# Wide column blocks in the query and gate rounds of an input projection, and one silu step for the gates

## The reference

```
h = rmsnorm(x, g_mix_pre)                       # (256, 2048)
proj = h @ w_in                                 # (2048, 8208)
mq, mk, mv, mo, mi, mf, rq, rk, rv, rg = split(proj)
mq, mk = silu(causal_dwconv(mq, mk))            # 8 mLSTM heads: convolution, silu
hm = mlstm(mq, mk, mv, mi, mf)                  # gate rows mi, mf: 8 columns each
hm = head_rmsnorm(hm, g_mlstm_head) * sigmoid(mo)
rq, rk = rotary(rq), rotary(rk)                 # 8 retention heads: rotated
hr = head_rmsnorm(retention(rq, rk, rv), g_ret_head) * silu(rg)
x = x + rmsnorm(concat(hm, hr) @ w_out, g_mix_post)
x = x + rmsnorm(swiglu_ffn(rmsnorm(x)), g_ffn_post)
```

## Time and profile before

| | |
|---|---|
| Median of 3 runs | 1235.89 us (1235.27 to 1236.32) |
| The profiled execution | 1238.89 us, of which the span of its instructions is 1237.2 us |
| PE busy | 1222.7 us, 99% of the span |
| DVE busy | 717.1 us, 58% |
| ACT busy | 599.3 us, 48% |
| DMA | 229.49 MB, mean 185 GB/s over the span |
| Mean granted clock of PE | 0.996 of full |

### The profile page before, as it was taken

One profiled execution on the slowest core, in us unless ns is written; L12 is line 12 of the kernel. 1 busy time (PEld: TensorE's weight loads), 2 busy tenths in 40 slices (PEclk: granted clock), 3 DMA queues, 4 the chain that ended last, 5 costly groups with the idle time before them and its releaser, 6 DMA issues.

```text
span 1237.2 us, 15798 instructions
## 1 busy us (share of the span) xinstructions
PE 1222.7 (99%) x5899; PEld 1026.1 (83%) x5899; DVE 717.1 (58%) x923; ACT 599.3 (48%) x789; POOL 14.2 (1%) x35
## 2 busy tenths in 40 slices
PE   8999999999999999999999999999999999999997
PEld 7888888888888888888888888888888888888886
DVE  6656778776777656744554554454455454544544
ACT  5654666574554645644444444444444444443442
POOL 2000100000000000000000000000000000000000
PEclk9999899999999999999999999999999999999999
DMA  8666798867887556465656565555656565556551
GB/s 313 208 145 165 132 213 171 146 166 163 204 179 187 200 178 214 157 193 181 194 180 203 175 198 190 183 192 184 200 173 200 188 220 203 182 192 204 186 188 69
DMA packets 136937, 229.49 MB, mean 185 GB/s; under 512 B 6080, under 2 KB 55488, under 8 KB 136384
## 3 DMA queue, kind: packets, MB, share of 16 engines
q1 hardware_dynamic: 136608, 226.84, 62.8%
q0 software_dynamic: 288, 2.10, 0.4%
HBM read 226.83 MB, written 2.10 MB: 185 GB/s over the span
## 4 chain that ended last, share of the span: by engine, by line
PE 90%; DMA 4%; DVE 3%; ACT 1%; issue 0%; SPq 0%; DVEq 0%; ACTq 0%
PE bank L1252 89%; DMA raw<-in_w_in 4%; DVE w_lo L779 1%; PE bank L1536 1%; DMA resid<-in_x 1%; ACT w_hi L441 1%; PE bank L1257 0%; PE bank L1454 0%; DVE gT L993 0%; ACT L604 0%; DVE h L806 0%; DVE resid L1124 0%; PE bank L1509 0%; DVE pre L966 0%; DVE hT L792 0%
## 5 line engine op out<-in xcount | busy, mean ns | idle before, releaser
L779 DVE TENSOR_TENSOR w_lo<-raw,w_hi 128x1024 fp32r<-128x1024 f32 x420 | 512.9, 1224 | 481.8 <-ACT w_hi L441 481.3
L441 ACT ACTIVATE w_hi<-raw 128x1024 fp32r<-128x1024 f32 x420 | 443.5, 1060 | 569.4 <-PE bank L1252 539.1
L1252 PE MATMUL bank<-w_hi,h2T 128*128 128x512 f32 x1376 | 426.6, 390 | 0.0
L1252 PEld LDWEIGHTS bank<-w_hi,h2T 128*128 128x128 f32 x1376 | 258.3, 188 | 53.4
L1252 PE MATMUL bank<-hT,w_hi 128*128 128x512 f32 x768 | 274.5, 401 | 0.0
L1252 PE MATMUL bank<-w_lo,h2T 128*128 128x512 f32 x688 | 267.7, 389 | 0.0
L1252 PE MATMUL bank<-w_hi,ffT 128*128 128x512 f32 x704 | 217.2, 389 | 0.0
L1252 PE MATMUL bank<-hT,w_lo 128*128 128x256 f32 x768 | 215.4, 280 | 0.0
L1252 PEld LDWEIGHTS bank<-hT,w_hi 128*128 128x128 f32 x768 | 145.5, 190 | 33.8 <-issue 0.2
L1252 PEld LDWEIGHTS bank<-w_hi,ffT 128*128 128x128 f32 x704 | 132.1, 188 | 27.3
L1252 PEld LDWEIGHTS bank<-w_lo,h2T 128*128 128x128 f32 x688 | 129.2, 188 | 26.5
(11 more groups left out here) (176 smaller groups left out, 566.4 us busy)
## 6 DMA issues: line engine op xcount, KB each, us to landing
raw<-in_w_in SPq DMA_DIRECT2D x63, 1024.0 KB, 12.8
raw<-in_w_gate SPq DMA_DIRECT2D x44, 1024.0 KB, 5.1
raw<-in_w_up SPq DMA_DIRECT2D x44, 1024.0 KB, 5.1
raw<-in_w_down SPq DMA_DIRECT2D x44, 1024.0 KB, 5.0
raw<-in_w_out SPq DMA_DIRECT2D x16, 1024.0 KB, 5.0
resid<-in_x SPq DMA_DIRECT2D x2, 1024.0 KB, 7.2
out<-resid SPq DMA_DIRECT2D x8, 256.0 KB, 2.5
raw<-in_w_in SPq DMA_DIRECT2D x2, 512.0 KB, 6.6
```

The costliest lines, as they stand in the source:

```text
L441: act.activation(w_hi[:, s % AHEAD, :], raw[:, s // 2, (s % 2) * SUB:(s % 2 + 1) * SUB], ACT.Copy).then_inc(hi_done, 1)
L779: dve.tensor_tensor(w_lo[:, s % AHEAD, :], raw[:, s // 2, (s % 2) * SUB:(s % 2 + 1) * SUB], w_hi[:, s % AHEAD, :].bitcast(F32), ALU.subtra ...
L1252: return pe.matmul(out_, lhsT, rhs, start=start, stop=stop, skip_group_check=True)
```

## The change

Query rounds and gate rounds are made "wide"; key rounds stay as they are. In a wide round a load fetches 4 k rows x 512 columns for each partition (runs of 2 KB), and one chunk serves both units. The eight steps take the pairs (unit, chunk) of `WIDE_ORDER`, so unit 0 ends at step 5 (before: 3) and unit 1 at step 7 (as before). Chunks 0 and 1 are first needed in steps 0 and 1 and free after steps 2 and 3, chunks 2 and 3 in steps 4 and 5 and free after 6 and 7; SP waits for `lo_done` accordingly (`WIDE_FREE`). PE first needs the banks of unit 1 at step 2 (before: 4).

`unit_at` follows the new ends. In ACT's `mixer_step` the silu of queries and keys now stands ahead of `copy_right`. For gates of retention heads ACT applies silu in one activation and DVE's multiplication is gone. The gate rows are worked up in another order: the sums that read bank 3 first, then the forget rows through to the absolute value, on which ACT's Exp waits, then the input rows.

```
+WIDE_ORDER = ((0, 0), (0, 1), (1, 0), (1, 1), (0, 2), (0, 3), (1, 2), (1, 3))
+WIDE_FREE = (3, 4, 7, 8)
+FREE = (2, 4, 6, 8)
+def is_wide(rnd):
+    return isinstance(rnd, int) and R_IN <= rnd < R_OUT and (rnd - R_IN) % 3 != 1
 def unit_at(rnd, s, lag):
     rnd, s = rnd - (lag > s), (s - lag) % 8
-    if R_IN <= rnd < R_OUT and s % 4 == 3:
-        return (*divmod(rnd - R_IN, 3), s // 4)
+    if R_IN <= rnd < R_OUT:
+        ends = (5, 7) if is_wide(rnd) else (3, 7)
+        if s in ends:
+            return (*divmod(rnd - R_IN, 3), ends.index(s))
     return None
...
+        def raw_sub(rnd, s):
+            if is_wide(rnd):
+                u, q = WIDE_ORDER[s]
+                return q, raw[:, q, :].rearrange("p (k c) -> p k c", c=512)[:, :, 256 * u:256 * u + 256]
+            return s // 2, raw[:, s // 2, (s % 2) * SUB:(s % 2 + 1) * SUB]
...
-                    sp.wait_ge(lo_done, 8 * (rnd - 1) + 2 * q + 2)
+                    sp.wait_ge(lo_done, 8 * (rnd - 1) + free[q])
...
-                            col = COL_RET * kind + 512 * half + (part * DH + (q // 2) * 256)
-                            load(6 * kind + 3 * half + (R_IN + n), q,
-                                 in_rows(8 * (q % 2), 8, col, 256))
+                            col = COL_RET * kind + 512 * half + part * DH
+                            if n == 1:
+                                src = in_rows(8 * (q % 2), 8, col + (q // 2) * 256, 256)
+                            else:
+                                src = in_rows(4 * q, 4, col, 512)
+                            load(6 * kind + 3 * half + (R_IN + n), q, src,
+                                 free=FREE if n == 2 else WIDE_FREE)
...
             def mixer_step(rnd, s):
+                ended = unit_at(rnd, s, 2)
+                if ended and ended[1] < 2:
+                    group, part, u = ended
+                    act.wait_ge(tiles_done, pair_of(group, part, u) + 1)
+                    act.activation((qT, kT)[part][:, 2 * u:2 * u + 2, :], new,
+                                   ACT.Silu if group < 2 else ACT.Copy).then_inc(pair_ready, 1)
                 ended = unit_at(rnd, s, 0)
                 if ended:
                     copy_right(ended[2], event_of(rnd, ended[2]))
...
-                    act.activation(new if group >= 2 else gT[:, two, :], gT[:, two, :], ACT.Sigmoid)\
+                    act.activation(gT[:, two, :], gT[:, two, :], ACT.Silu if group >= 2 else ACT.Sigmoid)\
                        .then_inc(gate_sig, 1)
...
-            for n, p0 in enumerate((0, 32)):
+            for p0 in (0, 32):
+                dve.tensor_tensor(row(R_Z)[p0:p0 + HEADS], bank[p0:p0 + HEADS, B_GATES, 0:SEQ],
+                                  row(R_RIGHT)[p0:p0 + HEADS], ALU.add).then_inc(gates_left, 1)
+            dve.wait_ge(gates_left, 2)
+            for n, p0 in enumerate((32, 0)):
                 z = row(R_Z)[p0:p0 + HEADS]
...
-                ended = unit_at(rnd, s, 2)
-                if ended and ended[0] >= 2 and ended[1] == 2:
-                    group, part, u = ended
-                    dve.wait_ge(gate_sig, 2 * group + u + 1)
-                    link(dve.tensor_tensor(gT[:, 2 * u:2 * u + 2, :], gT[:, 2 * u:2 * u + 2, :], new,
-                                           ALU.mult))
...
+            def wide_columns(rnd, event, act_T, before=None, after=None):
+                for s, (u, q) in enumerate(WIDE_ORDER):
+                    if q == 0:
+                        pe.wait_ge(acc_free, event + (u + 1))
+                    if before:
+                        before(s)
+                    sub_columns(rnd, s, act_T, u, q)
+                    if after:
+                        after(s)
...
-            pe.wait_ge(gates_act, 1)
-            pe.wait_ge(gates_dve, 2)
...
+            def gates_consumed(s):
+                if s == 2:
+                    pe.wait_ge(gates_act, 1)
+                    pe.wait_ge(gates_left, 2)
```

More of the change, by code:

```diff
@@ L263, in hybrid_layer @@
         gates_act = sem("gates_act")
+        gates_left = sem("gates_left")
         gates_dve = sem("gates_dve")
@@ L318, in _, with load @@
         def _(sp):
-            def load(rnd, q, src, wait=True):
+            def load(rnd, q, src, wait=True, free=FREE):
                 if wait:
-                    sp.wait_ge(lo_done, 8 * (rnd - 1) + 2 * q + 2)
+                    sp.wait_ge(lo_done, 8 * (rnd - 1) + free[q])
                 k = src.shape[1]
@@ L366, in _ @@
                         for q in range(4):
-                            col = COL_RET * kind + 512 * half + (part * DH + (q // 2) * 256)
-                            load(6 * kind + 3 * half + (R_IN + n), q,
-                                 in_rows(8 * (q % 2), 8, col, 256))
-            with sp.Fori(0, 4) as g:
+                            col = COL_RET * kind + 512 * half + part * DH
[5 more added lines that the diff above has]
+                                 free=FREE if n == 2 else WIDE_FREE)
+            for q in range(4):
+                load(R_OUT, q, rows(w_out, 4 * q, 4, 0, 512), free=WIDE_FREE)
+            with sp.Fori(1, 4) as g:
                 for q in range(4):
@@ L438, in hi @@
                 rnd, s = rnd + s // 8, s % 8
+                chunk, src = raw_sub(rnd, s)
                 if not first:
-                    act.wait_ge(raw_full[s // 2], 16 * (rnd + 1))
-                act.activation(w_hi[:, s % AHEAD, :], raw[:, s // 2, (s % 2) * SUB:(s % 2 + 1) * SUB],
-                               ACT.Copy).then_inc(hi_done, 1)
+                    act.wait_ge(raw_full[chunk], 16 * (rnd + 1))
+                act.activation(part_of(w_hi, rnd, s), src, ACT.Copy).then_inc(hi_done, 1)
             def early_hi(s):
@@ L927, in _ @@
             dve.wait_ge(gates_act, 1)
-            for n, p0 in enumerate((0, 32)):
+            for p0 in (0, 32):
[3 more added lines that the diff above has]
+            for n, p0 in enumerate((32, 0)):
                 z = row(R_Z)[p0:p0 + HEADS]
-                link(dve.scalar_tensor_tensor(z, row(R_LEFT_LO)[p0:p0 + HEADS], 1.0,
-                                              row(R_RIGHT_LO)[p0:p0 + HEADS], ALU.mult, ALU.add))
-                link(dve.tensor_tensor(z, z, row(R_RIGHT)[p0:p0 + HEADS], ALU.add))
-                link(dve.tensor_tensor(z, z, bank[p0:p0 + HEADS, B_GATES, 0:SEQ], ALU.add))
+                for lower in (R_LEFT_LO, R_RIGHT_LO):
+                    link(dve.tensor_tensor(z, z, row(lower)[p0:p0 + HEADS], ALU.add))
                 link(dve.tensor_tensor(z, z, rstd_row[p0:p0 + HEADS, :], ALU.mult))
-                gates(dve.tensor_scalar(z, z, vec[p0:p0 + HEADS, 2:3], None, ALU.add), n + 1)
-            gates(dve.scalar_tensor_tensor(rowf(R_ABS), rowf(R_Z), -1.0, rowf(R_Z), ALU.mult, ALU.max), 3)
+                gates(dve.tensor_scalar(z, z, vec[p0:p0 + HEADS, 2:3], None, ALU.add), 2 * n + 1)
+                if n == 0:
+                    gates(dve.scalar_tensor_tensor(rowf(R_ABS), rowf(R_Z), -1.0, rowf(R_Z), ALU.mult, ALU.max), 2)
             link(dve.memset(rowf(R_ONES), 1.0))
@@ L1485, in _ @@
                 gate_units(j, 3 * j + gate_round(0), 6 * j + event_of(gate_round(0), 0))
-                for n in (1, 2):
-                    for u in range(2):
-                        unit_columns(3 * j + (gate_round(0) + n), u,
-                                     6 * j + event_of(gate_round(0) + n, u), hT,
-                                     after=left_over(j) if n == 1 else None)
+                wide_columns(3 * j + (gate_round(0) + 1), 6 * j + event_of(gate_round(0) + 1, 0), hT,
+                             after=left_over(j))
+                for u in range(2):
+                    unit_columns(3 * j + (gate_round(0) + 2), u,
+                                 6 * j + event_of(gate_round(0) + 2, u), hT)
             gate_units(3, gate_round(3), event_of(gate_round(3), 0))
```

27 lines of the change are left out of this document (11 added, 16 removed).

## The result

| | us | range, executions |
|---|---|---|
| before | 1235.89 median | 1235.27 to 1237.51, 7 |
| after | 1241.29 median | 1240.99 to 1246.38, 7 |
| profiled execution of after | 1240.99 | span 1239.3 |

The change makes the kernel slower, by 5.4 us (0.44%) on the medians. Over all executions the ratio is 1.0057, 95% interval 1.0042 to 1.0071; among them are three of after that took 1243.3 to 1246.4 us. Profiled against profiled it is 1240.99 against 1238.89, +2.1 us. The two differ because the profiled execution of before stands 3.0 us over its median, that of after 0.3 us under it.

The account below looks back on a forecast made before the run. PE was taken as the bound, busy 1222.7 of 1237.2 us. Terms +7.4 + 0.8 - 2.5 - 0.8 - 3.4 = +1.5 us gave 1240.4 us for the profiled execution; the median forecast was 1238.6 us (+0.2%), range 1231 to 1245.

Parts of the forecast that it names:

- Part 4: End of the four gate rounds: ACT's gate activation, two steps later, makes PE wait 1.84 us each for y, +7.4 us.
- The +0.8 us for later heads: Gate rounds: y of head 3, behind another table load, comes 0 to 0.3 us late, 4 x 0.2 us.
- Part 1: Wide rounds: with 2 KB runs a load takes 5 to 7 us and PE's waits behind loads go, -2.5 us.
- a sign of being wrong: The prediction called itself wrong if, among other signs, loads of key rounds still take 20 us.
- The comparison with w_out: Median loads: w_in 12.8 us, w_out in 2 KB runs 5.0 us; w_out was the guide for wide-round loads.
- Rival 3: Loads: run length does not shorten them, the 2.5 us of waits stay, 1239.9 to 1243 us; chance 0.10.
- Part 2: Gate rows on DVE: the new order brings the column copy earlier, so PE's wait ahead of the spread goes, -0.8 us.
- Part 3: Around the spread: without the idle time ahead of the eight-row products the clock no longer falls, -3.4 us.
- two cases: Median: 1237.4 us if before's runs had the same late loads, 1239.9 if not; the middle, 1238.6, was taken.
- rival 1: Clock falls all the same, by eight-row products or in a new wait, 3.4 us each, 1240.8 to 1247 us; chance 0.24.
- Rival 2: Gate rounds: the new wait is short (0.56 us, or none) and the kernel faster, 1231.4 or 1229.2 us; chance 0.23.
- The chances for faster, same and slower: Whole kernel: faster (under 1233.4 us) 0.22, same 0.30, slower (over 1238.4 us) 0.48.

Follow-up runs that it names:

- gate_early: The changed kernel with ACT's activation of the gates ahead of the w_hi of the same step instead of behind it: 1231.16 us.
- queries_only: The changed kernel with the wide order in the query rounds alone, gate rounds loading and running 256 columns as before: 1236.40 us.
- table_first: The changed kernel with one extra one-column activation that loads the gates' table while ACT still waits for PE's step 6: 1235.91 us.
- runs_1k: gate_early with each load of a wide round issued as two of 512 KB, one for each 256 columns (1 KB runs): 1232.14 us.
- early_rows: The kernel before with DVE's new order of gate rows and ACT's gates' activation ahead of w_hi: 1233.06 us.
- rows_only: The kernel before with DVE's new order of gate rows alone: 1234.94 us.
- before_early: The kernel before with ACT's activation of the gates moved ahead of w_hi: 1234.55 us.
- spread_split: The changed kernel with the 16 eight-row products in two halves, behind the first and second steps of the key round: 1242.06 us.
- mix_later: The changed kernel with DVE's head_scaled (which makes y) ahead of mix (which waits for the gates): 1238.71 us.

## Why the prediction was right and wrong

**Part 4, the sign, was right.** Four waits of 1.84 us on y were forecast, 1.92 to 2.03 us came, with the same chain link by link. In the second gate round the sum is 0.13 us short. From the last y to PE's start I took 0.04 us, the link of a transpose; for weighted it is 0.24 us. From the activation to mix it is 0.11 us instead of 0.04, and PE ends step 7 0.17 us later behind w_hi than I had it, which hides most of it. The +0.8 us for later heads was not there: no wait at turned. 8.2 us forecast, 7.9 measured. gate_early and queries_only take the wait away, and table_first two thirds of it, each by another end of the mechanism.

**Part 1 was right in effect, half right in cause.** All three waits behind loads went in the profiled execution. But a query round's load takes 6.7 to 10.3 us (median 8.8) and a gate round's 6.9 to 17.1 (median 10.5), not 5 to 7. Loads of key rounds still take up to 20.3 us, which I had named as a sign of being wrong; in this execution they are hidden, in table_first two such loads cost PE 0.7 us. The comparison with w_out (5.0 us) blamed the run length for all of 7.8 us; runs_1k shows it to be the smaller share. That 512 B a run would do as well (the Trainium skill, DMA: Bandwidth & Descriptors, section Specifications) is not what these runs show at 1 KB, though it comes nearer to them than my term: 10.2 against 8.7 us a load, and no difference in time that can be told. Rival 3, with waits of 2.5 us kept, did not happen. How much of the 2.5 us the wide rounds are worth beyond one execution is open, since early_rows has no such wait without them.

**Part 2 was right.** Absolute value at 110.62 (forecast 110.4), copy at 131.42 (131.3), no idle time ahead of the spread. rows_only and before_early bear it out: the wait for floor goes in the one and stays (0.8 us) in the other.

**Part 3 failed.** The step was: "0.77 us idle and 2.47 us of eight-row products did not. After the change only the 2.47 us are left ... I take the fall as gone." The fall came without idle time in after, table_first, queries_only and early_rows, and did not come in before_early, whose spread follows an idle time:

```profile
133.22 2.13 PE L1257 MATMUL bank<-neg_m,sel_r 8*128 8x256 f32 x16 [0.79 <-DVE floor L963]
```

```profile
131.00:141.00 10.00, 9.21 (x57) 7.93 (x56) 8.81 (x17) 4.66 (x6) 0.00 (x0) 1.00 0.90 143
```

I had made a rule of two cases. In the fourteen profiled executions the fall came in two of the three with idle time ahead of the spread and in four of the eleven without. So the idle time does not decide it; the fall differs between executions of like code (after and gate_early have the same code up to this place). Five of the six last 3.41 us, which costs 1.7 us; the one that I priced lasts 6.83 us, twice as long. What sets a fall off stays open.

**From the profiled execution to the median.** This is the largest error. Against the profiled execution +1.5 us was forecast and +2.1 came, and that is in part luck: half the fall stayed (+1.7), the waits were 0.3 us less, and PE's faster pace in the last rounds (-0.8), which no part had, made up for the rest. On the median +2.7 was forecast and +5.4 came. 1241.29 us lies in the range of 1231 to 1245, but outside the forecast's own 1236.5 to 1240, in the stretch that I gave to rival 1. I gave two cases, "the median goes to 1237.4" or "to 1239.9", by whether its runs have the late loads. Both still counted the 3.4 us of the clock as there to be won in the median run. Both profiled executions of before stand 2.2 to 3.0 us over its medians, and single executions of it take as little as 1233.3 us. So most of its executions probably have less of both, though none of them was traced: they can't give back what they don't have. The new waits are fixed, 7.9 us in both profiled executions that have them (after, spread_split), and no execution of after took less than 1240.99 us. What the other parts are worth on the median is read from gate_early, 1231.2 to 1231.3 us: 3.8 to 5.0 us under before on the same chip, not 6.7.

**The rivals.** Rival 1 happened in part: the clock fell, at a price of 1.7 and not 3.4 us, and spread_split shows one 1.5 us behind the end of a new wait. Executions of after at 1243.3, 1245.1 and 1246.4 us, with granted clocks of 0.997, 0.995 and 0.994, fit one to three further falls, though no trace of these was taken. Rival 2 did not happen, but was priced well: "if this runs while ACT waits for PE's step 6, the wait is 1.84 - 1.28 = 0.56 us". table_first made it so and has 2.2 us in four waits.

The chances for faster, same and slower are added up slightly wrong: by the parts given they are 0.21, 0.30 and 0.49.

The drain of about 1.38 us that the Trainium skill adds to each table load (ScalarE: Activation LUTs, section What ACT_TABLE_LOAD costs) is not in the trace: the activation starts 0.02 us behind the end of the load, and taking the load away gave 5.4 us for four, where load and drain together would be an estimated 10.6 by that section's figures.

## What to carry to other kernels

When a change lets a pair of tiles end later within a round, follow what stands behind each converting step on the engine that frees the next weights: here one activation, with its table load, behind a w_hi that waits for the last step but one, cost 8 us, and its place one instruction earlier gave them back and made the change pay (1231.2 against 1236.1 us; 1.7 us less than the kernel before with both new orders). Put work whose input is there ahead of the instruction that waits for the busy engine. What a profiled execution shows as lost to the clock or to a late load may not be in the median run. Price a gain from it by how often it occurs, and a new fixed wait in full, or somewhat over it.

## What the runs showed of the hardware

**PE has two paces in the same loop.** Stretches of steps with the same 16 products at full clock take 2.77 or 2.83 us a step, and keep the pace until the next product of another kind or wait. The two rows of gate_early's chain above show it: 32 products of the same shapes in 5.55 us, and 5.65 us behind the transpose at 260.98. mix_later is at the slower pace in three groups of rounds, before in its last three. Per 13 steps it is 0.7 us, so comparisons below 1 us need this looked at. What sets the pace is open.

**A fall of the clock can come and stay away in like executions.** Leaving out the last 6 us of each span, the fourteen traces have eight falls, none more than one to a trace. Seven lasted 3.41 us and one 6.83, at 0.50. Six began between 134.6 and 135.8 us, one at 163.9 (rows_only, 0.2 us behind the end of a wait of 2.53 us) and one at 260.9 us (spread_split). Waits of 1.65 us in before and of four times about 1.97 us in after had none behind them.

**A wait costs PE more than the idle time shown.** Products of this kind start 0.11 to 0.12 us apart though a row gives each 0.28 us. Behind the wait of 1.97 us in after 2.14 us are lost.
